# Down weights loaded as four neighbouring rows to a partition, 64 partitions to a transfer

## The reference, cut to what matters

```
for e in range(N_EXPERTS):                      # 8 experts
    out = out + combine[:, e:e + 1] * swiglu(t, w_gate[e], w_up[e], w_down[e])
# swiglu(h, g, u, d) = (silu(h @ g) * (h @ u)) @ d
# w_gate, w_up: 8 x 1024 x 3584;  w_down: 8 x 3584 x 1024
```

## Time and profile before

| | |
|---|---|
| Median of 3 runs | 1441.28 us (1438.74 to 1442.69) |
| Profiled execution | 1441.36 us, of which the profile's span is 1439.7 us |
| Mean granted TensorE clock | 0.998 of full speed |
| TensorE matmuls | busy 97% of the span |
| DVE / ACT / GpSimd | busy 33% / 21% / 8% |
| Moved by DMA | 456.23 MB, on average 317 GB/s |

### The profile page before, as it was taken

How to read it: one execution, slowest core, us unless ns; L and a number is a source line. 1 busy time by engine, 2 the same in 40 slices (tenths; PEclk the granted TensorE clock), 3 DMA queues, 4 the chain that set the end, 5 groups by cost and what they waited for, 6 DMA issues and landing times.

```text
span 1439.7 us, 34819 instructions
## 1 busy us (share of the span) xinstructions
PE 1403.3 (97%) x15324; PEld 893.0 (62%) x15324; DVE 468.5 (33%) x932; ACT 299.1 (21%) x570; POOL 122.3 (8%) x158
## 2 busy tenths in 40 slices
PE   8999999999999999999999999999999999899898
PEld 6987789999997973564564353353354345344345
DVE  5698666666445840021021021021021002101102
ACT  5544564444445550000000000000000000000000
POOL 3644000000000024001000000000000000000100
PEclk9999999999999999999999999999999999999999
DMA  7561994255554349999999999999999999999995
GB/s 252 214 239 61 386 331 163 88 191 199 196 185 158 117 171 343 386 408 391 404 405 392 405 403 399 399 389 400 398 396 408 391 386 409 390 392 408 394 393 234
DMA packets 149997, 456.23 MB, mean 317 GB/s; under 512 B 12677, under 2 KB 15803, under 8 KB 149851
## 3 DMA queue, kind: packets, MB, share of 16 engines
q1 hardware_dynamic: 142448, 439.61, 79.5%
q0 software_dynamic: 3888, 11.31, 2.9%
q10 hardware_dynamic: 3514, 3.08, 0.7%
HBM read 442.86 MB, written 11.11 MB: 315 GB/s over the span
## 4 chain that ended last, share of the span: by engine, by line
PE 48%; SPq 43%; DMA 4%; issue 3%; DVE 1%; ACT 1%; DVEq 0%; ACTq 0%
SPq L741 30%; PE bank L2010 26%; SPq L748 12%; PE bank L2539 9%; PE bank L2554 6%; DMA ring<-in_moe_w_down 3%; PE bank L2215 1%; DMA ring<-in_attn_w_in 1%; PE bank L2227 1%; PE bank L2189 1%; PE bank L2308 0%; SPq L687 0%; PE bank L2249 0%; PE bank L2172 0%; PE bank L2270 0%
## 5 line engine op out<-in xcount | busy, mean ns | idle before, releaser
L2539 PE MATMUL bank<-ring,xg 128*32 128x512 f32 (+1 forms) x6144 | 587.0, 539 | 10.4 <-DMA ring<-in_moe_w_up 7.3
L2539 PEld LDWEIGHTS bank<-ring,xg 128*32 128x32 f32 x6144 | 220.4, 110 | 360.7 <-issue 294.6
L2554 PE MATMUL bank<-ring,heT 128*32 128x256 f32 x5280 | 293.0, 381 | 13.6 <-DMA ring<-in_moe_w_down 13.5
L2554 PEld LDWEIGHTS bank<-ring,heT 128*32 128x32 f32 x5280 | 194.8, 111 | 117.5 <-DMA ring<-in_moe_w_down 16.8
L1895 DVE TENSOR_TENSOR he<-he,bank 128x256 f32<-128x256 f32 (+1 forms) x96 | 31.6, 383 | 492.5 <-ACT he L1341 472.6
L1341 ACT ACTIVATE he<-bank 128x256 f32<-128x256 f32 (+1 forms) x93 | 26.6, 357 | 774.9 <-PE bank L2539 774.9
L2010 PE MATMUL bank<-hL_r,wd 128*128 128x288 f32 x480 | 142.7, 297 | 0.0
L1413 DVE TENSOR_TENSOR ring_r<-ring,wd 128x1024 fp32r<-128x1024 f32 x90 | 110.0, 1225 | 69.6 <-ACT wd L997 67.8
L997 ACT ACTIVATE wd<-ring 128x1024 fp32r<-128x1024 f32 x90 | 95.1, 1059 | 133.9 <-PE bank L2010 133.9
L2010 PE MATMUL bank<-hU,wd 128*128 128x288 f32 x352 | 103.9, 295 | 0.0
L2010 PE MATMUL bank<-hU,ring_r 128*128 128x288 f32 x352 | 103.0, 293 | 0.0
(11 more groups left out here) (440 smaller groups left out, 1325.5 us busy)
## 6 DMA issues: line engine op xcount, KB each, us to landing
ring<-in_moe_w_gate SPq DMA_DIRECT2D x112, 1024.0 KB, 14.5
ring<-in_moe_w_up SPq DMA_DIRECT2D x112, 1024.0 KB, 19.8
ring<-in_moe_w_down SPq DMA_DIRECT2D x112, 1024.0 KB, 13.7
ring<-in_attn_w_in SPq DMA_DIRECT2D x6, 2048.0 KB, 13.0
ring<-in_ffn_w_gate SPq DMA_DIRECT2D x5, 2048.0 KB, 16.2
ring<-in_ffn_w_up SPq DMA_DIRECT2D x5, 2048.0 KB, 9.1
ring<-in_cache_k SPq DMA_DIRECT2D x16, 512.0 KB, 8.4
ring<-in_cache_v SPq DMA_DIRECT2D x16, 512.0 KB
```

What stands on the lines that cost most here:

```text
L2539: last = mm(out, xg[:, k, GRP * r:GRP * r + GRP], w[:, :, j, :, q, :], start=(k == 0), stop=(k == KD - 1), skip_group_check=True)
L2554: last = mm(sums_of(r)[GRP * q:GRP * q + GRP, :], left, w[:, j, 256 * cols_:256 * cols_ + 256], start=first, stop=(c == NCH - 1 and j == C ...
```

## The change

Three places change together.

A down tile is loaded by two transfers still, of 1 MB each. Partition p now holds the four neighbouring rows 4p, 4p + 1, 4p + 2 and 4p + 3 of the block of 512, which are 16 KB in one piece in HBM and in the partition. The first transfer writes partitions 0 to 63, the second 64 to 127.

In `gated` the columns of a group `q` are now 128 neighbouring columns of each 512, not four runs of 32.

In `turned` a block of 32 x 32 is now made of every fourth column of the product, so that unit 4p + m of a block of 512 lands on partition p in the m-th block.

```diff
             else:
-                pairs = a["moe_w_down"][0].rearrange("e (c f) d -> (e c) f d", f=CH // 2)
-                at = (FROM[c] // CH + h) * 2
+                blocks = a["moe_w_down"][0].rearrange("e (c f) d -> (e c) f d", f=CH)
+                src = blocks[bass.ds(e * (DFE // CH) + (FROM[c] // CH + h), 1), :, :]
+                rows = src.rearrange("o (p m) d -> p (o m d)", m=CH // P)
                 for part in range(2):
-                    src = pairs[bass.ds(e * (2 * DFE // CH) + (at + part), 1), :, :]
-                    sp.dma_start(ring[s][:, SLOT // 2 * part:SLOT // 2 * part + SLOT // 2].rearrange("p (k f) -> p k f", k=2),
-                                 src.rearrange("o (k p) f -> p (o k) f", p=P)).then_inc(got, 16)
+                    half = slice(P // 2 * part, P // 2 * part + P // 2)
+                    sp.dma_start(ring[s][half, :], rows[half, :]).then_inc(got, 16)
...
-                last_turn = v.transpose(out=dst[:, 0:n // GRP, GRP * r:GRP * r + GRP],
-                                        in_=he[:, r, 0:n].rearrange("p (b f) -> p b f", f=GRP))
+                last_turn = v.transpose(out=dst[:, 0:n // GRP, GRP * r:GRP * r + GRP].rearrange("p (b m) s -> p b m s", m=4),
+                                        in_=he[:, r, 0:n].rearrange("p (b f m) -> p b m f", f=GRP, m=4))
...
-            w = ring[expert_slot(g)][:].rearrange("p (two k b q f) -> p two k b q f", two=2, k=ks, q=4, f=GRP)
+            w = ring[expert_slot(g)][:].rearrange("p (two k b q f) -> p two k b q f", two=2, k=ks, q=4, f=P)
...
-                        out = pair_banks(c)[r][GRP * q:GRP * q + GRP, 0:2 * n].rearrange("p (two b f) -> p two b f", two=2, f=GRP)
+                        out = pair_banks(c)[r][GRP * q:GRP * q + GRP, 0:2 * n].rearrange("p (two b f) -> p two b f", two=2, f=P)
```

## The result

The changed kernel takes 1882.28 us at the median (1860.17 to 1889.06, 5 runs), against 1441.28. The ratio is 1.302, with a 95% interval from 1.294 to 1.311; it compares the means of the fast runs, without the one of 1889.06 us, which counts as a slow one. Its profiled execution is the quickest of the five, 1860.17 us with a span of 1858.5, so differences taken from the profile are some 20 us smaller than those of the medians. I had forecast 1680, and no more than 1765.

A forecast was written before the change was run, and what follows sets the result against it. The prediction took the expert stage to be bound by transfers, TensorE 1 to 2% behind. 1441 + 240 us for half-partition down loads, with issues, TensorE, turns and clock at 0, made 1681, given as 1680; range 1425 to 1765.

The forecast's parts named there:

- What bounds the kernel: Expert stage: bound by transfers, TensorE 1 to 2% behind; a faster down load gives at most about 24 us.
- Size of pieces: Down loads: 16 KB pieces take 596 ns where four of 4 KB take 646, saving 22 us of DMA time.
- rival B: Down loads: engines a transfer apart write opposite halves, no piece is slowed; 1426 us, between 1419 and 1437; chance 0.20.
- Half of the partitions, the price: Down loads: a tile whose transfers find all engines in the same half takes 10.0 us, 267 us more over 56.
- The row of `x_sample`: Load at the start, 32 partitions of 4 KB: engines busy but at 188 to 205 GB/s, a bound for narrow transfers.
- Half of the partitions, the nine tenths: Down loads: some engines will be a transfer apart, so nine tenths of 267 us is taken, 240 us.
- My top end: Range's upper end, 1765 us; all down tiles at 11.2 us would give 1774, and that top was left out.
- Issues on SyncE: Queue of SyncE: as many instructions as before, 0.37 us for an unhindered issue, not the bound: 0.
- TensorE: Expert stage matmuls: same number and shapes, gated operand read in runs of 128 columns instead of 32: 0.
- Turns: Transposes on DVE: reading every fourth element takes at most four times the time, hidden by TensorE's work: 0.
- The clock: TensorE's clock after waits within down tiles: lowering hidden by nearly 5 us of slack a tile: 0, up to a few tens.
- The marks: Expert stage signs: rate near 200 alternating with 400 GB/s, DMA share 1.0, down waits over 200 us, 43,000 fewer packets.

The follow-up runs named there:

- wide16: The changed kernel, but each down tile is loaded by one 2 MB transfer over all 128 partitions, in the same 16 KB pieces: 1436.14 us, ratio 0.9953.
- light_half: The changed kernel with all its transfers, but nearly three quarters of the expert stage's matmuls left out: 1877.85 us, ratio 1.303.
- allhalf: The changed kernel, with the gated tiles also loaded by neighbouring halves of the partitions, in four transfers each: 2025.31 us, ratio 1.404.
- evenodd: The changed kernel, but the first down transfer writes the even partitions and the second the odd ones: 1434.81 us, ratio 0.9952.
- wide8: The changed kernel, but each down transfer writes all 128 partitions, two rows of each, in 8 KB pieces: 1435.02 us, ratio 0.9954.

## Why the prediction was wrong

*What bounds the kernel*: right. The stage follows its transfers, and the narrow load came out in full.

*Size of pieces*: right in mechanism, but the saving was put twice too high. The piece took 622 ns for 596, and since four of 4 KB take 646, the saving is 24 ns and not 50, 11 us of DMA time and not 22. So 0.5% came of it, 1435 us for the 1426 of rival B; in the changed kernel it is drowned.

*Half of the partitions, the price*: right. I took 10.0 us for a down tile with its engines in step; it is 9.7. The row of `x_sample`, 188 to 205 GB/s in the earlier trace rows, was the one that told it.

The Trainium skill's rule that I had set beside it (SBUF — State Buffer, section "Door 1: The DMA port swizzle (why `[64,N]` ≈ `[32,N]`)") holds here in the part that tells most: not how many partitions a transfer writes, but how many ways in they reach. By its table, even and odd partitions reach all 16 ports each, and that run is as fast as one over all 128, 1434.8 us for the 1436.1 of `wide16`.

*Half of the partitions, the nine tenths*: this step failed, and the forecast with it. I wrote that some engines would be apart, and reckoned that being apart can only relieve. What the runs showed in its place: an engine that is still loading a down half while another has gone on to full gated transfers slows that one too (its pieces of 4 KB take 286 ns and more, where 165 is usual, once five down pieces are in flight), 100 us where 20 are spared, and what falls behind holds up SyncE's queue until the others stand idle, another 76 us. In step, with a queue that stays full, the kernel would have taken some 1435 + 267 = 1702 us, an estimate from these runs that no run reached; I forecast 1680. By this estimate the difference to the 1882 is the engines' falling apart. That 1680 lies near this estimate does not make the nine tenths right: they took something off for engines out of step, where the runs added 156 us (80 and 76). My top end went wrong for the same reason: it took the dearest rate for down tiles only, and nothing for gated ones.

*Issues on SyncE*: I put them at 0. The instruction itself is cheap, but as a single queue for all sixteen engines it is where two late engines hold up all sixteen, as from 1097.5 to 1100.5 us. That step was wrong, by some 76 us.

*TensorE*: right; three kernels with the new columns are as fast as the layout before or faster. *Turns*: right that they are hidden. The strided read takes 631 ns for the 417 of the earlier trace rows, one and a half times, where I had allowed up to four:

```profile
L1902 DVE STREAM_TRANSPOSE heT<-he 128x256 f32<-128x256 f32 x69 | 39.9, 631 | 268.9 <-PE bank L2554 268.9
```

*The clock*: right at 0, by `light_half`.

*The rivals*: B, engines a transfer apart that don't disturb each other, gets its purest form in `allhalf`, and falls: 2025 us. It is true in part there, 3.5 us a tile and not 5.

*The marks*: the share of TensorE, 82%, and the rate near 200 in stretches came as written; that the DMA share would stay at 1.0 did not, and its fall to 0.89 is the mark of the second loss. Packets became fewer by 21,505, and 56 x 384 are 21,504; I had written 43,000, twice that, by a slip. I looked for the waits before down matmuls, over 200 us; they are 116, and 207 lie before gated ones. That should be read as the sign that unchanged transfers suffer.

What stays open: how an engine first falls behind, which ones do, and which of them meet. The views don't tell engines apart. That an engine alone at a down tile is slowed too (939 ns) can explain why one that is behind falls further behind, but this is argued, not shown. No run takes away the idle time by itself.

## What to carry to other kernels

Choose the partitions of a narrow transfer by where they lie: even and odd ones cost nothing here, neighbouring halves doubled each of their pieces, with the DMA engines as busy as ever while they were in step, so look at GB/s beside the DMA share. When transfers of two kinds follow each other through one queue, price not only the slow kind but what it does to the other: here a narrow tile cost 4.8 us of its own and 8 to 10 in all, and a short stretch at the rate of one or two engines, beside a long issue on the queue, is its mark. The version to keep is `evenodd`, or as good `wide8` and `wide16`, 0.5% faster than before.

## What the runs showed that I had not expected

A wait that costs 177 us in one kernel gained 90 in the other, as it kept the engines in step. A single narrow tile in 21 costs 10 us, more than each of seven. And a kernel in which every transfer is narrow pays less than half as much for each tile as one in which a third of them is.
